# Hybrid decoder step with a routed mixture of experts: the third token tile of the gather in two row halves, half of the first expert product ahead of the branch, and fetched expert rows requested and added later

## The reference, cut to what matters

```python
combine = jnp.sum(jax.nn.one_hot(expert, N_EXPERTS) * weights[..., None], axis=1)   # two non-zero per token
h1 = jnp.einsum('td,edf->tef', t, w1)          # 16 experts, 1024 -> 512
h3 = jnp.einsum('td,edf->tef', t, w3)
act = jax.nn.silu(h1) * h3 * combine[:, :, None]
y = jnp.einsum('tef,efd->td', act, w2)         # 512 -> 1024
h = h + gate2 * y                              # then the next sub-layer, or the last RMSNorm
```

## Time and profile before

| | |
|---|---|
| median of 3 runs | 1045.85 us (1040.45 to 1045.91) |
| the profiled execution: its own time, span | 1042.76 us, 1040.9 us |
| TensorE busy | 977.2 us, 94% of the span |
| VectorE, ScalarE busy | 325.5 us, 174.8 us |
| moved by DMA | 316.24 MB, mean 304 GB/s |
| mean granted TensorE clock | 0.965 of full speed |

### The profile page before, as it was taken

How to read it: one execution, slowest core, us unless ns; L and a number is a source line. 1 busy time by engine, 2 the same in 40 slices (tenths; PEclk the granted TensorE clock), 3 DMA queues, 4 the chain that set the end, 5 groups by cost and what they waited for, 6 DMA issues and landing times.

```text
span 1040.9 us, 13295 instructions
## 1 busy us (share of the span) xinstructions
PE 977.2 (94%) x5418; PEld 555.8 (53%) x5418; DVE 325.5 (31%) x831; ACT 174.8 (17%) x388; POOL 40.0 (4%) x68
## 2 busy tenths in 40 slices
PE   6999999999799979999999979999989999999976
PEld 3666655584374655444443536777665444443533
DVE  3241123306541361112110117738552111211025
ACT  2200000003321231111110202055222111101112
POOL 0000000001320000000000200000000000000200
PEclk9999999989889999999999989999999999999989
DMA  9945778728981838999999993214856999999971
GB/s 379 373 162 188 263 277 323 310 94 301 401 344 67 358 129 339 407 422 422 422 422 421 407 403 116 94 68 162 343 228 252 398 422 421 422 421 422 419 278 51
DMA packets 47624, 316.24 MB, mean 304 GB/s; under 512 B 5602, under 2 KB 6002, under 8 KB 12354
## 3 DMA queue, kind: packets, MB, share of 16 engines
q1 hardware_dynamic: 39456, 288.90, 68.9%
q0 software_dynamic: 6096, 22.30, 5.6%
q10 hardware_dynamic: 2002, 4.08, 1.0%
HBM read 303.84 MB, written 11.42 MB: 303 GB/s over the span
## 4 chain that ended last, share of the span: by engine, by line
PE 75%; DMA 10%; SPq 8%; DVE 4%; issue 1%; ACT 1%; DVEq 0%; ACTq 0%
PE banks L795 25%; PE banks L1373 14%; SPq L413 8%; DMA ring<-in_ew 7%; PE banks L1426 7%; PE banks L1352 6%; PE banks L872 4%; DMA ring<-in_w 3%; PE banks L912 2%; PE banks L859 1%; PE banks L1443 1%; PE banks L1389 1%; PE banks L981 1%; PE banks L1465 1%; PE banks L804 1%
## 5 line engine op out<-in xcount | busy, mean ns | idle before, releaser
L795 PE MATMUL banks<-uT,ring 128*128 128x320 f32 x448 | 125.2, 439 | 2.6 <-DVE uT L1636 2.6
L1373 PE MATMUL banks<-ring,scr 128*64 128x512 f32 x480 | 108.3, 601 | 5.7 <-issue 5.0
L795 PEld LDWEIGHTS banks<-uT,ring 128*128 128x128 f32 x448 | 85.9, 193 | 43.3 <-issue 8.2
L1373 PE MATMUL banks<-scr 128*64 128x512 f32 x416 | 95.9, 611 | 5.0 <-DMA scr<-in_ew 5.0
L1352 PEld LDWEIGHTS banks<-scr 128*128 128x128 f32 x768 | 88.3, 192 | 12.8 <-issue 12.8
L1352 PE MATMUL banks<-scr 128*128 128x128 f32 x768 | 92.1, 277 | 0.0
L1373 PEld LDWEIGHTS banks<-ring,scr 128*64 128x64 f32 x480 | 35.3, 138 | 74.9 <-issue 69.6
L607 ACT ACTIVATE scr<-banks,mods 128x128 f32<-128x128 f32 x128 | 36.5, 368 | 183.3 <-PE banks L1352 183.3
L1373 PEld LDWEIGHTS banks<-scr 128*64 128x64 f32 x416 | 31.4, 140 | 66.4 <-issue 59.7
L795 PE MATMUL banks<-ring,uT 128*128 128x512 f32 x128 | 57.0, 598 | 0.0
L795 PE MATMUL banks<-scr,ring 128*128 128x320 f32 x192 | 52.9, 433 | 1.4 <-DVE scr L2398 1.4
(11 more groups left out here) (389 smaller groups left out, 1024.3 us busy)
## 6 DMA issues: line engine op xcount, KB each, us to landing
ring<-in_ew SPq DMA_DIRECT2D x96, 1024.0 KB, 20.5
scr<-in_ew SPq DMA_DIRECT2D x96, 1024.0 KB, 20.8
ring<-in_w SPq DMA_DIRECT2D x80, 1024.0 KB, 8.3
scr<-in_v POOLq DMA_DIRECT2D x16, 256.0 KB, 9.6
yd<-uT POOLq DMA_DIRECT2D x8, 512.0 KB, 8.6
scr<-in_kT POOLq DMA_DIRECT2D x13, 256.0 KB, 9.1
out_hgrn<-scr SPq DMA_DIRECT2D x1, 2304.0 KB, 18.1
scr<-in_s POOLq DMA_DIRECT2D x1, 2048.0 KB, 9.9
```

Source lines behind the costliest of these rows:

```text
L795: last = mm(out, a, b, start=(first and i == 0), stop=(final and i == len(pairs) - 1))
L1373: ins = mm(ps[bank][SLOTS * x:SLOTS * x + SLOTS, :], xe[:, kk, SLOTS * x:SLOTS * x + SLOTS], wab[SLOT[n]][:, x, kk % 4, :], start=(kk == 0 ...
```

## The change: what it does

1. The third token tile: feature blocks 0 to 3 of the 64 sample tokens stay in partitions 0 to 63, blocks 4 to 7 go to partitions 64 to 127 (`half_rows`). The zeros are gone. The matmuls of this tile use 64 rows each and alternate between the row halves and between banks 1 and 0. They now come at the end of gather half 0, eight of them; gather half 1 keeps eight matmuls of 128 rows. The last `tokens` tile is a plain matmul with the identity instead of a transpose; VectorE copies one column of `rcol` and of `slot` to the other half.
2. `first_half`: the four feature blocks of piece 0 times `xe` run before the branch; after it `hidden` goes on with piece 1 (and gives slot 0 back there). In `dense`, which uses bank 2 later, two more matmuls close the bank.
3. GpSimd asks for the rows when h1 of pair 7 is done and piece 46 has landed, tile order 2, 0, 1.
4. `turn_rows` is split: tile 2 between `outputs_last` and `add_last`, tiles 0 and 1 after `add_last`. ScalarE and VectorE follow: tile 2 before their copy of pair 7's output, tiles 0 and 1 after it.

```diff
-        ROWS_ORDER = (0, 1, 2)
+        ROWS_ORDER = (2, 0, 1)
+        def half_rows(i):
+            return slice(NS_TOK * i, NS_TOK * i + NS_TOK)
# GpSimd, expert_rows
-                pool.wait_ge(sem(f"xe_ps{l}"), 2 * NPAIR)
+                pool.wait_ge(sem(f"h1_ps{l}"), NPAIR)
+                n = AT_MOE[l] + MOE_PIECES - 2
+                pool.wait_ge(sem(f"piece_in{SLOT[n]}"), 32 * (ROUND[n] + 1))
# ScalarE, routed
-                for t in ROWS_ORDER:
-                    first_rows(t)
+                first_rows(2)
                 expert_out(NPAIR - 1)
+                first_rows(0)
+                first_rows(1)
# TensorE, tokens (o is the bank)
-                    last = pe.transpose(o[0:rows, P * d:P * d + P], uT[:, d0 + d, P * t:P * t + rows], ident)
+                    x = uT[:, d0 + d, P * t:P * t + TROWS[t]]
+                    last = pe.transpose(o[r, P * d:P * d + P], x, ident) if n < 5 else mm(o[r, P * d:P * d + P], x, ident, start=True, stop=True)
# TensorE, gather
-                for d in range(4 * half, 4 * half + 4):
-                    for t in range(TT):
-                        ins = mm(ps[half][:, PAIR * (d % 4):PAIR * (d % 4) + PAIR], utok[:, t, P * d:P * d + P],
-                                 pick[:, t, :, :].rearrange("p e n -> p (e n)"), start=(t == 0), stop=(t == TT - 1))
-                        give(ins, f"xe_ps{l}" if d % 4 == 3 and t == TT - 1 else None)
+                def part(h, j, t, first=False, final=False):
+                    d, r = 4 * h + j, slice(0, P) if t < 2 else half_rows(h)
+                    ins = mm(ps[h][:, PAIR * j:PAIR * j + PAIR], utok[r, t, P * d:P * d + P],
+                             pick[r, t, :, :].rearrange("p e n -> p (e n)"), start=first, stop=final)
+                    give(ins, f"xe_ps{l}" if final else None)
+                for j in range(4):
+                    for t in range(2):
+                        part(half, j, t, half == 0 and j == 0 and t == 0, half == 1 and j == 3 and t == 1)
+                if half == 0:
+                    for j in range(4):
+                        part(1, j, 2, j == 0)
+                        part(0, j, 2, False, j == 3)
+            def first_half(l):
+                n = AT_MOE[l]
+                piece(n)
+                pe.wait_ge(sem(f"xe_ev{l}"), 1)
+                for kk in range(4):
+                    for x in range(2):
+                        give(mm(ps[2][SLOTS * x:SLOTS * x + SLOTS, :], xe[:, kk, SLOTS * x:SLOTS * x + SLOTS],
+                                wab[SLOT[n]][:, x, kk, :], start=(kk == 0), stop=False))
# TensorE, hidden
-                    for h in range(2):
+                    if q == 0 and i == 0:
+                        used(at)
+                    for h in range(1 if q == 0 and i == 0 else 0, 2):
# TensorE, end of routed
                 hidden_last(1, 3, "h3_ps")
-                turn_rows()
                 turn(NPAIR - 1)
                 outputs_last()
+                turn_rows(2)
                 add_last(NPAIR - 1)
+                turn_rows(0)
+                turn_rows(1)
# TensorE, experts
                 gather(l, 0, 1)
+                first_half(l)
                 pe.wait_ge(sem("over_ready"), 2 * l + 1)
# VectorE
-                v.memset(utok[64:P, 2, :], 0.0).then_inc(sem("utok_zero"), 1)
+                cp(rcol[half_rows(1), 2:3], rcol[half_rows(0), 2:3])
+                step(cp(slot[half_rows(1), 2, 0:NE], slot[half_rows(0), 2, 0:NE]))
-                    if q == NPAIR - 1:
-                        for t in ROWS_ORDER:
-                            both_rows(t)
+                    if q == NPAIR - 1:
+                        both_rows(2)
                     expert_out(q)
+                both_rows(0)
+                both_rows(1)
```

More of the change, by code:

```diff
@@ L492, in _ @@
             pool.wait_ge(sem("h_ready"), 2 * DT)
+            pool.wait_ge(sem("rows_in1"), 32)
             pool.dma_start(hist, I["convT"]).then_inc(sem("rows_in1"), 16)
@@ L687, in shifts_out @@
                 e.wait_ge(sem("bias_ps"), 3 + 2 * l + i)
-                e.copy(shifts[0:NS_TOK, 512 * i:512 * i + 512], ps[(3 if l == 0 else 4) + i][0:NS_TOK, :]).then_inc(sem("bias_ev"), 1)
+                e.copy(shifts[half_rows(i), 512 * i:512 * i + 512], ps[(3 if l == 0 else 4) + i][half_rows(i), :]).then_inc(sem("bias_ev"), 1)
             def spread_out(s):
@@ L1191, in shift_tokens @@
                 for j in range(4):
-                    last = mm(bank[0:NS_TOK, P * j:P * j + P], srep[l][:, 4 * i + j, :], ident, start=True, stop=True)
+                    last = mm(bank[half_rows(i), P * j:P * j + P], srep[l][:, 4 * i + j, :], ident, start=True, stop=True)
                 last.then_inc(sem("bias_ps"), 1)
@@ L1302, in dense @@
                 pe.wait_ge(sem(f"xe_ev{l}"), 2)
+                for x in range(2):
+                    mm(ps[2][SLOTS * x:SLOTS * x + SLOTS, :], xe[:, 0, SLOTS * x:SLOTS * x + SLOTS],
+                       wab[SLOT[AT_MOE[l]]][:, x, 0, :], start=False, stop=True)
                 mm(ps[7][:, 0:T], ident[:, RW:RW + 1].broadcast_to([P, P]), lr[:, 0:T], start=True, stop=False)
@@ L1305, in dense @@
                 pe.wait_ge(sem(f"rows_ready{l}"), 4)
-                mm(ps[7][:, 0:1], ones[:, :], ones[:, 0:1], start=True, stop=True).then_inc(sem(f"xe_ps{l}"), 2 * NPAIR - 3)
                 for p in range(NPAIR):
@@ L1314, in tokens @@
                 t, d0 = n // 2, 4 * (n % 2)
-                rows, o = TROWS[t], ps[TOKEN_BANK[n]]
+                r, o = slice(0, P) if t < 2 else half_rows(n % 2), ps[TOKEN_BANK[n]]
                 for d in range(4):
-                    last = pe.transpose(o[0:rows, P * d:P * d + P], uT[:, d0 + d, P * t:P * t + rows], ident)
+                    x = uT[:, d0 + d, P * t:P * t + TROWS[t]]
+                    last = pe.transpose(o[r, P * d:P * d + P], x, ident) if n < 5 else mm(o[r, P * d:P * d + P], x, ident, start=True, stop=True)
                 last.then_inc(sem("utok_ps"), 1)
@@ L1348, in gather @@
                         pe.wait_ge(sem("utok_ev"), 6 * l + 6)
-                        pe.wait_ge(sem("utok_zero"), l + 1)
-                for d in range(4 * half, 4 * half + 4):
-                    for t in range(TT):
-                        ins = mm(ps[half][:, PAIR * (d % 4):PAIR * (d % 4) + PAIR], utok[:, t, P * d:P * d + P],
-                                 pick[:, t, :, :].rearrange("p e n -> p (e n)"), start=(t == 0), stop=(t == TT - 1))
-                        give(ins, f"xe_ps{l}" if d % 4 == 3 and t == TT - 1 else None)
+                def part(h, j, t, first=False, final=False):
[15 more added lines that the diff above has]
+                for kk in range(4):
+                    for x in range(2):
+                        give(mm(ps[2][SLOTS * x:SLOTS * x + SLOTS, :], xe[:, kk, SLOTS * x:SLOTS * x + SLOTS],
+                                wab[SLOT[n]][:, x, kk, :], start=(kk == 0), stop=False))
             def routed(l):
@@ L1456, in turn_back, with turn_rows @@
                         give(ins, f"back_ps{l}" if t == TT - 1 else None)
[L1458 to L1465, removed]
+                def turn_rows(t):
+                    r = TROWS[t]
+                    pe.wait_ge(sem(f"rows_ready{l}"), ROWS_ORDER.index(t) + 1)
+                    for i, m in enumerate(SUM_ORDER):
+                        o = sum_p(m)[:, P * t:P * t + P] if t < 2 else sum_s[:, m, :]
+                        last = t == ROWS_ORDER[-1] and i % 2 == 1
+                        give(mm(o, yrows0[t][0:r, P * m:P * m + P], ident[0:r, 0:r], start=False, stop=last), f"out_ps{l}" if last else None)
                 def chunk_of(q, m):
@@ L1501, in add_last @@
                     for i, m in enumerate(SUM_ORDER):
-                        give(mm(sum_p(m), chunk_of(q, m), back[1][:, 0:NP_TOK], start=False, stop=(i % 2 == 1)),
-                             f"out_ps{l}" if i % 2 else None)
+                        give(mm(sum_p(m), chunk_of(q, m), back[1][:, 0:NP_TOK], start=False, stop=False))
                 for q in range(NPAIR - 1):
@@ L1686, in tokens @@
                 t, c = n // 2, slice(512 * (n % 2), 512 * (n % 2) + 512)
-                rows = TROWS[t]
                 if n == 4:
@@ L1690, in tokens @@
                 v.wait_ge(sem("utok_ps"), 6 * l + n + 1)
-                stt(utok[0:rows, t, c], ps[TOKEN_BANK[n]][0:rows, :], rcol[0:rows, t:t + 1], shifts[0:rows, c], MUL, ADD)\
+                r = half_rows(n % 2)
+                stt(utok[r, t, c], ps[TOKEN_BANK[n]][r, :], rcol[r, t:t + 1], shifts[r, c], MUL, ADD)\
                     .then_inc(sem("utok_ev"), 1)
@@ L1854, in both_rows @@
                     v.wait_ge(sem(f"rows_in{t}"), ROWS_BEFORE[t][l] + 32 * (l + 1))
-                    v.wait_ge(sem(f"product_ready{l}"), t + 1)
+                    v.wait_ge(sem(f"product_ready{l}"), ROWS_ORDER.index(t) + 1)
```

## The result

The changed kernel is faster: 1033.78 us against 1043.19 (medians of 15 runs each), ratio 0.9907 with a 95% interval of 0.9885 to 0.9928, so 9.7 us. Forecast were 18.8, to 1027 us. The profiled execution has a span of 1035.5 us, 5.4 less than before.

The account below looks back on a forecast made before the run. The prediction took the expert stages to be bound by the weight stream. It summed -13.2 (rows and layer end), -0.9 (last gather) and -4.7 (start of experts) to -18.8 us, from 1045.85 to 1027 us, range 1018 to 1038.

Parts of the forecast that it names:

- The rows leave the stream: Last pieces of each layer: without 2.62 MB of rows, piece 45 lands sooner; h3 done 8.3 and 8.7 us earlier.
- The end of the layer: After h3 of pair 7: `turn_rows` moves behind the last product, no stall for rows; 21.1 us in place of 19.8.
- The gather: Third token tile's matmuls: row halves overlap by half, 0.45 us less per gather, three gathers counting in each layer.
- Rival 1: Gather and branch: row halves overlap fully and the branch stall is hidden; 24.1 us faster, 1022 us; chance 0.2.
- Start of the experts: Gather to piece 8: `first_half` ahead of the branch; with two gathers, 3.2 us saved in layer 0, 1.5 in layer 1.
- Rival 2: Layer end: rows delay piece 47 and themselves, each layer losing 3.5 to 4 us; 1034 to 1036 us; chance 0.15.
- Rival 3: Piece 45 is held by a slot, not the stream, so the row transfer was hidden anyway; 1044 us; chance 0.07.
- Rival 4: Layer end: fetching rows is slow by itself, 27 us from request to last landing; slower, 1053 us; chance 0.08.

Follow-up runs that it names:

- early_ask: The changed kernel, but with the rows asked for after the last gather, as before the change; ratio to the kernel before 0.9981.
- tail_only: The kernel before with only parts 3 and 4 of the change, the late row request and the split `turn_rows`; ratio 0.9894.
- no_halves: The changed kernel without part 1, so the third token tile is whole as before; ratio to the kernel before 0.9898.
- warm_start: The changed kernel with nine filler matmuls in TensorE's wait for the router, ahead of the expert counts; ratio to the kernel before 0.9928.
- nh_ask_45: no_halves with the rows asked for once piece 45 has landed, not piece 46; ratio to the kernel before 0.9938.

## Why the prediction was right in direction, and half in size

*The rows leave the stream*: right, and to size. From the start of pair 6's h3 to the end of pair 7's it fell by 9.0 and 9.7 us (forecast 8.3 and 8.7, and 0.45 for the gather in between), TensorE became the bound, and early_ask puts the waits back.

*The end of the layer*: this is the step that failed in size. Forecast was +1.3 us from h3's end to the last add, 21.1 in place of 19.8. The four kernels with late rows and no fillers at the end (changed, tail_only, no_halves, warm_start) have 21.2 to 28.7 in eight layers, 24.0 in the mean: +4.2. Two terms of the sum were too small. I sized the fetch at 400 GB/s, from a stream of weights; with the stream almost gone it moved 210 to 291 GB/s in windows of 5 us. So tile 2 was 8.1 and 10.2 us behind h3's end, where I had taken 5 to 8, and TensorE waited 0.6 and 1.5 us. The larger term is the clock: I had priced all matmuls of this stretch at full clock, though it now has four short idle stretches within 11 us in layer 0 and three within 13 us in layer 1. In layer 0 the lower clock cost 1.7 us (the second part of `add_last` 5.32 against 3.67), in layer 1 6.7 (5.34, 3.06, 3.67 and 5.89 against 3.64, 2.00, 2.00 and 3.67). Where neither came, in no_halves' layer 0, the end took 21.2 us, about what was forecast. VectorE's last part also ends 0.8 us later behind TensorE, 0.6 forecast. By parts 3 and 4 alone, 13.2 us were forecast; tail_only gained 11 by its ratio and by its rows, the clock that comes back in h3 with it, and 7.4 ± 1.3 at equal clock.

*The gather*: half an overlap was taken. The gather went from 5.52 to 5.02 us; the rows of one kind, by line and shape, are

```profile
L1363 PE MATMUL banks<-scr 128*128 128x128 f32 x512 | 64.0, 278 | 0.0
L1363 PE MATMUL banks<-scr 64*128 64x128 f32 x256 | 18.6, 285 | 0.0
```

0.125 us for each instruction of 128 rows and 0.073 of 64: the halves do run beside each other, but not two in the time of one (0.063). Rival 1 fell on this. The Trainium skill (TensorE: Matmul & The Clock Gate, table on small-K matmuls) says that row groups run concurrently; the trace agrees that they do, at 1.7 times. On the clock it gained nothing: part 1 is worth 0.6 ± 1.0 us.

*Start of the experts*: half of the branch was taken as hidden (1.3 us left); 0.73 and 0.75 stayed. From gather to piece 8 the gain was even larger than forecast, 3.9 and 2.0 us. What failed is what I put ahead of it, +0.3 and +0.5: it was +3.5 and +2.1. Part 1's eight instructions in place of four are about 1 us of this at the lower clock (2.94 us for the last two token tiles, x12, in place of 1.89, x8, in tail_only). The rest is the clock itself, which I had read from one execution: the kernel before had it full there in layer 0 and not in layer 1, tail_only in neither.

Rival 2 (rows come later than taken, 1034 to 1036) is nearest to the 1033.8 measured; of its two halves the rows came late and piece 47 did not (0.32 us of idle in layer 0, none in layer 1; the most in any profile is 1.57, in warm_start's layer 1). Rival 3 fell with tail_only. Rival 4, a fetch that takes 27 us by itself, fell: it takes 13.8 and 14.7.

Of the 18.8 us, 11.2 came at equal clock, and the mean clock fell from 0.9665 to 0.9643, which by the slope costs 1.6. Whether the change or chance lowered it, 15 runs can't tell. The time of 1033.8 lies 6.8 us above the forecast and inside its range because the range was wide: its start, 1045.85, was a median of three runs, 2.7 above that of 15, and the 5 us that I took for the scatter are 15.

## What to carry to other kernels

Read the end of a stream-bound stage backwards: what shares the stream ahead of the last piece and isn't needed before it (here 2.62 MB; 8 to 9 us in each layer) is worth its whole transfer there, while the work of its consumers must find a place where TensorE isn't left idle in small pieces. Price every matmul behind such gaps at the lower clock too, and fill a known wait with no more matmuls than it is long: four fillers in a wait of 2.8 us took no_halves from 0.9898 to 0.9825, while nine overran it. Where the clock scatters from run to run, compare kernels at equal clock too, or gains that add look as if they did not; and look in the rows whether an edit moves the clock itself, for that part is missing at equal clock.

## What the runs showed of the hardware that I had not expected

- Time against mean granted clock: 0.71 us for each 0.001 over 221 runs of 14 kernels, and 1.6 us of scatter around it.
- Fetched rows of 4 KB, alone on the queues, moved 211 GB/s at a DMA share of 1.04 (998 to 1000) and 363 GB/s at 0.99 in the next 2 us, once GpSimd's last request was out; weights at such a share move 420.
- The lower clock came after idle stretches of 0.9 to 1.5 us in the changed kernel's layer 1, and not at once after the same 0.88 and 0.98 in layer 0 (`outputs_last` 3.64 and 3.64 us there, the second part of `add_last` 5.32).
- VectorE began a product 3.3 us after its operand in both layers, 1.6 us after the last of GpSimd's indirect DMAs was issued (nh_ask_45); the cause is open.
